# Turned exponents of an attention stage loaded back from device memory once a query block, not once a query head

## What is computed

```python
def attend_block(args):          # n: one of 4 query blocks of 128 tokens
    ...
    s_win = jnp.einsum('bqkgd,bjkd->bkgqj', qn, kw).astype(jnp.float32) * scale
    s_ctx = jnp.einsum('bqkgd,bjkd->bkgqj', qn, k_ctx).astype(jnp.float32) * scale
    ...
    logits = jnp.concatenate([sink_logits(sink, s_win.shape[:-1]), s_ctx, s_win], axis=-1)
    p = jax.nn.softmax(logits, axis=-1)
    ...
    return (jnp.einsum('bkgqj,bjkd->bqkgd', p_ctx, v_ctx)
            + jnp.einsum('bkgqj,bjkd->bqkgd', p_win, vw))
```

## Time and profile before

| | us |
|---|---|
| median of 3 runs | 1403.59 |
| lowest and highest | 1402.69, 1404.76 |
| the profiled execution, its own time | 1405.84 |
| its span from first to last instruction | 1404.1 |
| TensorE busy in it | 1367.9 (97%) |
| DVE busy | 864.5 (62%) |
| ScalarE busy | 517.5 (37%) |
| TensorE's waits in the whole span, for pt_lo and for q_lo | 9.3 and 2.1 |

### The profile page before, as it was taken

The page is one execution under the profiler, slowest core; times in us unless marked ns, Lnnn a source line. Parts: engine busy times, 40 slices in busy tenths (PEclk is TensorE's granted clock), DMA queues, the critical chain, the costliest instruction groups (busy, mean ns, idle before and its releaser), DMA issues.

```text
span 1404.1 us, 19111 instructions
## 1 busy us (share of the span) xinstructions
PE 1367.9 (97%) x7258; PEld 1142.4 (81%) x7258; DVE 864.5 (62%) x1327; ACT 517.5 (37%) x798; POOL 74.8 (5%) x145
## 2 busy tenths in 40 slices
PE   5999999999999999999999999999999999999998
PEld 2788888888878788878888888888888888887887
DVE  6545655656787787776645776677665334474435
ACT  5323422234564645454222442212363223333332
POOL 0001111111000000000110100000000000010000
PEclk9999999999999999999999999999999999999999
DMA  9996567666676757687766666356533333365333
GB/s 384 407 396 250 180 206 254 191 186 198 201 208 163 192 172 178 176 230 261 236 198 192 195 192 194 92 173 195 160 91 102 103 91 105 105 198 181 111 90 120
DMA packets 103490, 265.35 MB, mean 189 GB/s; under 512 B 13536, under 2 KB 41200, under 8 KB 102000
## 3 DMA queue, kind: packets, MB, share of 16 engines
q1 hardware_dynamic: 81792, 185.72, 42.5%
q0 software_dynamic: 19936, 73.38, 16.7%
q10 hardware_dynamic: 1680, 5.10, 1.0%
HBM read 245.78 MB, written 18.38 MB: 188 GB/s over the span
## 4 chain that ended last, share of the span: by engine, by line
PE 83%; DMA 6%; DVE 5%; issue 2%; SPq 2%; ACT 2%; DVEq 0%; ACTq 0%
PE ps L1578 83%; DMA blocks<-cond_row 2%; DMA modchunk<-blocks 2%; DMA kvmem<-in_ctxT 1%; SPq L431 1%; DVE w_lo L972 1%; DVE pt_lo L1288 1%; DMA raw<-in_mod 1%; ACT w_hi L543 1%; DVE cond_row L1275 1%; DVE tmp L1265 0%; SPq L389 0%; DVE tmp L1098 0%; DVE kvmem L1160 0%; DVE kvmem L1265 0%
## 5 line engine op out<-in xcount | busy, mean ns | idle before, releaser
L1578 PE MATMUL ps<-h_hi,w_hi 128*128 128x512 f32 x1592 | 621.0, 390 | 2.1 <-DVE h_lo L1053 1.2
L1578 PE MATMUL ps<-h_lo,w_hi 128*128 128x512 f32 x1592 | 618.5, 389 | 0.0
L1578 PE MATMUL ps<-h_hi,w_lo 128*128 128x512 f32 x1592 | 618.2, 388 | 0.0
L972 DVE TENSOR_TENSOR w_lo<-raw,w_hi 128x1024 fp32r<-128x1024 f32 x206 | 252.2, 1224 | 371.2 <-ACT w_hi L543 370.3
L543 ACT CAST w_hi<-raw 128x1024 fp32r<-128x1024 f32 x206 | 216.1, 1049 | 598.8 <-PE ps L1578 598.7
L1578 PEld LDWEIGHTS ps<-h_hi,w_hi 128*128 128x128 f32 x1592 | 299.0, 188 | 65.8 <-issue 5.4
L1578 PEld LDWEIGHTS ps<-h_hi,w_lo 128*128 128x128 f32 x1592 | 298.9, 188 | 62.0
L1578 PEld LDWEIGHTS ps<-h_lo,w_hi 128*128 128x128 f32 x1592 | 299.0, 188 | 58.5
L978 DVE CUSTOM_DVE_ANT_0 modchunk<-modchunk,cond_row 128x1024 f32<-128x1024 f32 x128 | 154.6, 1219 | 19.9 <-DMA modchunk<-in_modb 19.7
L489 POOL DMA_DIRECT2D modchunk<-in_modb x128 | 67.6, 528 | 828.3 <-DVE modacc L978 811.9
L744 ACT ACTIVATE tmp<-tmp,stat 128x513 f32<-128x513 f32 (+1 forms) x24 | 18.7, 780 | 43.1 <-DVE stat L1265 43.0
(11 more groups left out here) (231 smaller groups left out, 1356.1 us busy)
## 6 DMA issues: line engine op xcount, KB each, us to landing
raw<-in_weights SPq DMA_DIRECT2D x208, 512.0 KB, 3.6
modchunk<-in_modb POOLq DMA_DIRECT2D x128, 512.0 KB, 4.7
raw<-in_mod SPq DMA_DIRECT2D x32, 512.0 KB, 9.2
modchunk<-in_mod SPq DMA_DIRECT2D x16, 512.0 KB, 7.5
cond_row<-in_mod SPq DMA_DIRECT2D x16, 512.0 KB, 9.5
blocks<-cond_row SPq DMA_DIRECT2D x24, 320.0 KB, 5.4
blocks<-cond_row SPq DMA_DIRECT2D x24, 256.0 KB, 2.9
modchunk<-blocks SPq DMA_DIRECT2D x64, 80.0 KB, 3.6
```

The source lines that it names most:

```text
L972: nc.vector.tensor_tensor(low, src, high.bitcast(F32), ALU.subtract).then_inc(lo_ready, 1)
L1578: return nc.tensor.matmul(out, lhsT, rhs, start=start, stop=stop, skip_group_check=True)
```

## The change

The three query heads of a block share one fetch. The stores stay one a head, now into a scratch area laid out so that a row of one partition group holds all three heads: a store writes 512 runs of 512 or 640 B instead of 128 rows of 2048 or 2560 B. Behind the third store of a block stand four loads, each of 128 rows of 1536 or 1920 B, into one landing buffer that takes up to 1920 of `modchunk`'s 2048 columns. The inverse rows move to the part of `cond_row` that a landing buffer held.

The high parts of a block's three heads are cast together in slots 4, 7, 10 and 13 (`HIGH_SLOTS`), the low parts together in slots 5, 8, 11 and 14 (`LOW_SLOTS`). The product with the values stays in slots 6, 9, 12 and 15. GpSimd's load of the conditioning row now waits for the last `block_out`.

```diff
-TURN_LAG = 3
-TURN_SLOTS = 3
+HIGH_SLOTS = (4, 7, 10, 13)
+LOW_SLOTS = (5, 8, 11, 14)
...
-        blocks_in = [cond_row[:, 2 * most:3 * most], chunk_flat[:, 0:most], chunk_flat[:, most:2 * most]]
-        inverse_rows = [chunk_flat[:, 2 * most + b * GQA * P:2 * most + (b + 1) * GQA * P] for b in range(2)]
+        inverse_rows = [cond_row[:, 2 * most + b * GQA * P:2 * most + (b + 1) * GQA * P] for b in range(2)]
...
-        def landed_tiles(i, k):
-
-            return blocks_in[(i * STEPS + k) % TURN_SLOTS][:, 0:key_tiles(k) * P].rearrange("p (a t c) -> p t a c", a=4, c=QUADRANT)
+        def landed_tiles(k):
+
+            run = key_tiles(k) * QUADRANT
+            landed = chunk_flat[:, 0:4 * GQA * run].rearrange("p (a x) -> p a x", a=4)
+            return landed[:, :, k % GQA * run:(k % GQA + 1) * run].rearrange("p a (t c) -> p t a c", c=QUADRANT)
...
+            def scratch_block(n, i):
+                run = key_tiles(n * GQA) * QUADRANT
+                return turn_scratch[(i * BLOCKS + n) % 2, 0:P * 4 * GQA * run].rearrange("(p j h x) -> p j h x", j=4, h=GQA, x=run)
+
             def store_blocks(i, k):
-                g, cols = i * STEPS + k, key_tiles(k) * P
+                g, run = i * STEPS + k, key_tiles(k) * QUADRANT
                 sp.wait_ge(turned, g + 1)
-                sp.dma_start(turn_scratch[g % 4, :, 0:cols], blocks_out[g % 2][:, 0:cols]).then_inc(written[g % 2], 16)
-
-            def fetch_blocks(i, k):
-                g, cols = i * STEPS + k, key_tiles(k) * P
-                run, slot = cols // 4, g % TURN_SLOTS
-                sp.wait_ge(written[g % 2], 16 * (g // 2 + 1))
-                if g >= TURN_SLOTS:
-                    sp.wait_ge(pt_ready, g + 1 - TURN_SLOTS)
+                sp.dma_start(scratch_block(k // GQA, i)[:, :, k % GQA],
+                             blocks_out[g % 2][:, 0:4 * run].rearrange("p (j x) -> p j x", j=4)).then_inc(written[g % 2], 16)
+
+            def fetch_blocks(i, n):
+                b, run = i * BLOCKS + n, key_tiles(n * GQA) * QUADRANT
+                for parity in range(2):
+                    sp.wait_ge(written[parity], 16 * ((GQA * (b + 1) + 1 - parity) // 2))
+                if b:
+                    sp.wait_ge(pt_ready, b * GQA)
                 for j in range(4):
-                    sp.dma_start(blocks_in[slot][j * QUADRANT:(j + 1) * QUADRANT, 0:cols].rearrange("c (a x) -> c a x", a=4),
-                                 turn_scratch[g % 4, :, j * run:(j + 1) * run].rearrange("(a c) x -> c a x", a=4)
-                                 ).then_inc(pt_landed[slot], 16)
+                    sp.dma_start(chunk_flat[j * QUADRANT:(j + 1) * QUADRANT, 0:4 * GQA * run].rearrange("c (a x) -> c a x", a=4),
+                                 scratch_block(n, i)[:, j].rearrange("(a c) h x -> c a (h x)", a=4)).then_inc(pt_landed, 16)
...
-                    if 1 <= k <= STEPS and (k > 1 or i == 0):
-                        fetch_blocks(i, k - 1)
                     if k < STEPS and k % GQA == GQA - 1:
                         store_inverse(i, k // GQA)
+                        fetch_blocks(i, k // GQA)
...
-            pool.wait_ge(pt_ready, KV_HEADS * STEPS)
+            pool.wait_ge(y_done, KV_HEADS * BLOCKS)
             pool.dma_start(cond_row[:], row_scratch.broadcast_to([P, D])).then_inc(row_back, 16)
-            pool.wait_ge(y_done, KV_HEADS * BLOCKS)
...
-                    if TURN_LAG <= k < STEPS + TURN_LAG:
-                        turned_hi(i, k - TURN_LAG)
+                    if k in HIGH_SLOTS:
+                        for j in range(GQA):
+                            turned_hi(i, HIGH_SLOTS.index(k) * GQA + j)
...
-                    if k > TURN_LAG:
-                        for n in {NEXT_SCORES: (STEPS - 2, STEPS - 1), NEXT_SCORES + 1: ()}.get(k, (k - TURN_LAG - 1,)):
-                            turned_lo(i, n)
+                    if k in LOW_SLOTS:
+                        for j in range(GQA):
+                            turned_lo(i, LOW_SLOTS.index(k) * GQA + j)
```

More of the change, by code:

```diff
@@ L353, in build @@
         written = [sem(f"written{i}") for i in range(2)]
-        pt_landed = [sem(f"pt_landed{i}") for i in range(TURN_SLOTS)]
+        pt_landed = sem("pt_landed")
         inverse_ready = sem("inverse_ready")
```

15 lines of the change are left out of this document (7 added, 8 removed).

## The result

The changed kernel takes **1447.23 us** (median of 4 runs, 1445.88 to 1449.39) against 1403.80 (median of 4 runs): 3.1% slower, ratio 1.0311, 95% interval 1.0293 to 1.0329. The prediction said 1401.8 and at most 1415. The profiled execution took 1446.46 us, its span 1444.8.

The account below looks back on a forecast made before the run. TensorE, busy 97%, was taken as the bound, so only its waits could give time back. Heads summed to -0.3 - 0.8 - 2.4 + 1.7 = -1.8 us, from 1403.59 to 1401.8 us; range 1394 to 1415.

Parts of the forecast that it names:

- 1.3 + 2.2 + 0.9 = 4.4 us from first issue to last landing (3.6 to 6.5 kept): Fetch of a block: 1.3 us across four issues, 2.2 us for a small load's landing, 0.9 us for the larger size.
- The 0.9: Fetch of a block: extra microseconds until the last load lands, because each load carries three times the bytes.
- the model block: Block 1 of the second KV head (steps 3 to 5, 640 columns), followed slot by slot and then carried to other heads.
- 2.7 us (2.1 to 3.6): Third store of a block, in 512 runs: time to land, with no weight load issued in the 5 us ahead.
- the wait of 0.8: Second head: new TensorE wait of 0.8 us, as step 9's scores need q_lo, made behind three casts and two swaps.
- The break-even is at 7.4 us: Store and fetch together: 7.4 us would leave the time unchanged; each microsecond beyond costs 8 us; 7.2 us was forecast.
- win 0.3, 0.8 and 2.4 and lose 1.7: Attention stage, heads one to four: microseconds won in the first three and lost in the fourth, -1.8 us in all.
- the slower rival: Attention stage: data land late, store and fetch 8.2 us give +6.6 us, 9.5 us some +17; chance 0.27.
- that wait never comes last: Single landing buffer: a fetch's wait for the previous block's low parts was claimed to cost nothing.
- the reload of cond_row: GpSimd's load after the last block_out: 3 us later, landed by some 658 us, 4 us of cover before its reader.
- The marks of "right": Attention-stage waits and landings expected in the trace if the forecast of -1.8 us held.
- ScalarE's casts waiting over 2 us: Sign that the forecast is wrong: ScalarE's casts wait over 2 us for a landing in the attention stage.

## Why the prediction was wrong

**What bounds the kernel.** This was right: TensorE's waits, and low parts behind a maximum. Making two low parts earlier cut the waits for pt_lo from 9.3 to 2.6 us and gave 5.3 us, with no transfer changed.

**The step that failed first: "1.3 + 2.2 + 0.9 = 4.4 us from first issue to last landing (3.6 to 6.5 kept)".** It is 7.3 us on average to the cast, beyond the range. The 0.9 was read from 512 KB weight loads, which fill 128 partitions, and stood for one load, not for four. Even a third of the bytes took 4.7, not 3.5; all of them took 6.0 over 128 partitions and 7.3 over 32. The Trainium skill (SBUF — State Buffer, section "Door 1: The DMA port swizzle") gives about 218 GB/s as the most that 32 partitions take, and its section "The DMA setup-cost knee" a fixed 2 us. An estimate by these, if the four loads go one after another, is 960 KB / 218 = 4.5 us plus 2, so 6.5 us from the first issue; the model block took 7.2.

**The store, "2.7 us (2.1 to 3.6)".** It took 3.4 us on average to the first load's issue, 4.1 in the model block and 2.6 at the least. The form of 512 runs is in that least value, 2.6 for 2.0; what the rest waits for was not taken apart.

**The landing of the model block.** By its own steps: from q_lo to the turn's end 2.6 us (measured 481.92 less 479.36, 2.6); TensorE wants step 9's scores 13.3 us behind that q_lo (497.79 less 5.15 is 492.64: 13.3); casts 2.0, swap 1.3, q_hi 0.5 as read. Only store and fetch, forecast at 7.2, took 11.4, which is 4.2 more, and the wait of 0.8 became 5.15, which is 4.35 more. The place of the new wait, q_lo at step 9 behind three casts and the swaps, was right.

**"The break-even is at 7.4 us, and beyond it each microsecond costs 8."** The line through three kernels puts it at 7.2, so in this order of work the length of store and fetch decided the sign. The slope is 12, not 8. I let delays fade from head to head and within a head except in the fourth. Measured from first product to first product, the first three heads grew by 6.8, 8.4 and 6.2 us, and the fourth, to its last product, by 15.3; the forecast had them win 0.3, 0.8 and 2.4 and lose 1.7, and even the slower rival gave the fourth 6.5. The sentence that hid it: "those stand in DVE's order ahead of the very turn whose store the fetch needs, so that wait never comes last". The observation was right and the conclusion beside the point: low parts ahead of that turn close a loop from one block's landing to the next's. From 434 to 660 us the chain of work runs around it all but without TensorE, so a head takes as long as the loop's rounds (73.7 us in the second) and not as long as TensorE needs (65.3). Opening it on both engines gave back 28.5 us; on DVE alone 2.7, within the noise.

**The slower rival** had the place and the sign, and the mechanism but for the loop, at a chance of 0.27, with 8.2 and 9.5 us as its sizes. The measured 10.7 would have been some +26 by its own price, against +43.4. One of its sums is off as well: by the prediction's own steps, 8.2 us make the wait at step 9 1.8 us and not 2.2.

**Smaller terms.** Loads once a block took 128 issues off SyncE; what this is worth by itself was not run. No wait for the reload of cond_row stands on DVE (it was issued at 689.28 us, with a wait of 1.2 us for a chunk load behind it). The marks of "right" (pt_lo under 4, q_lo 4 to 6, landing 6 to 8 us behind the store's issue, ScalarE's wait under 1) all failed; "ScalarE's casts waiting over 2 us" came true in thirteen of sixteen blocks, stores over 3.6 us in six, and the fourth head was longer by 15.3 us where over 4 was the sign.

**Open:** what the store's form costs inside the loop; how the fourth head's loss divides between splits and the load of x; what opening ScalarE's order alone would give; and how much the fixed part of the fetch owes to stores and weight loads beside it.

## What to carry to other kernels

Before lumping transfers, follow one round from landing to landing through every engine's program order. If no row of the bounding engine is in it and the rounds together are longer than what that engine needs, their length sets the time. A transfer's size must be priced with the partitions that it fills, from a row of the same target. And where a wait is for work in the wrong order, move the work: two low parts of each head made earlier won 5 us, where 128 saved loads lost 43.

## What was unexpected of the hardware

- Four loads of the same bytes: 7.3 us to the cast into 32 partitions each, 6.0 over 128. A plain order of memory won nothing (1451.2 us against 1447.2).
- A load whose memory side begins with a dimension of 4 ran at some 100 GB/s, with two tenths of the DMA engines' time busy, and cost the kernel 114 us.
- The granted clock fell to 0.93 to 0.98 over 70 us windows once waits of up to 6.4 us came into the stage. Bringing it back to 0.98 to 1.00 by dummy products won nothing (1448.1 us against 1447.2), since the loop set the time.
- A store of 512 runs took 525 ns to issue where one of 128 rows took 338. With nothing ahead it landed in 2.6 us for 2.0; behind other traffic the medians are the same.
